# Rotary neighbours by a partition shuffle on VectorE instead of TensorE products

## The reference

```
x <- LN(alpha*x + 1/2*(1+g1)*SwiGLU_1(x*(1+s1)+b1))
x <- LN(alpha*x + (1+g2)*W_o[MoBA heads | GLA heads](x*(1+s2)+b2))
x <- LN(alpha*x + 1/2*(1+g3)*SwiGLU_2(x*(1+s3)+b3))
```

```
half = 8
x1, x2 = xr[..., :half], xr[..., half:]           # xr = x[..., :16]
rot = concat([x1*cos - x2*sin, x2*cos + x1*sin])  # features 16..63 unchanged
```

## Time and profile before

| what | us |
|---|---|
| median of 3 runs | 903.28 |
| the profiled execution | 907.4 |
| its span on the core | 905.6 |
| TensorE busy | 861.6 (95%) |
| VectorE busy | 551.8 (61%) |
| ScalarE busy | 348.0 (38%) |
| input product, first row of MI+1 to last row of level 5 | 326.6 to 421.3 |

### The profile page before, as it was taken

One profiled execution on the slowest core, in us unless ns is written; L12 is line 12 of the kernel. 1 busy time (PEld: TensorE's weight loads), 2 busy tenths in 40 slices (PEclk: granted clock), 3 DMA queues, 4 the chain that ended last, 5 costly groups with the idle time before them and its releaser, 6 DMA issues. The chain is left out here.

```text
span 905.6 us, 17041 instructions
## 1 busy us (share of the span) xinstructions
PE 861.6 (95%) x6857; PEld 756.3 (84%) x6857; DVE 551.8 (61%) x873; ACT 348.0 (38%) x494; POOL 27.8 (3%) x32
## 2 busy tenths in 40 slices
PE   5999999999999999999998999979999999999994
PEld 2488988898999589998666777768699999999993
DVE  1454445455566599685786655763877765555656
ACT  2333333223434455354556443621443223334341
POOL 0000000000000000000000000000200000000002
PEclk9799999999999999999999999989999999999997
DMA  9989888987856563546999999989536555534521
GB/s 318 339 259 290 264 246 243 271 254 200 250 162 201 174 202 96 188 147 200 383 317 330 380 386 340 337 316 275 145 106 174 140 142 155 140 97 134 155 64 58
DMA packets 209028, 200.96 MB, mean 222 GB/s; under 512 B 9601, under 2 KB 161293, under 8 KB 208822
## 3 DMA queue, kind: packets, MB, share of 16 engines
q1 hardware_dynamic: 207556, 196.04, 69.4%
q0 software_dynamic: 704, 2.49, 0.7%
q10 hardware_dynamic: 690, 1.35, 0.5%
HBM read 196.04 MB, written 3.80 MB: 221 GB/s over the span
## 5 line engine op out<-in xcount | busy, mean ns | idle before, releaser
L792 PE MATMUL B<-Hh,wh 128*128 128x320 f32 x864 | 258.9, 313 | 0.1
L1841 DVE TENSOR_TENSOR wl<-raw,wh 128x2048 fp32r<-128x2048 f32 x90 | 206.7, 2298 | 85.7 <-ACT wh L1457 85.4
L793 PE MATMUL B<-Hl,wh 128*128 128x320 f32 x864 | 255.0, 309 | 0.0
L1457 ACT ACTIVATE wh<-raw 128x2048 fp32r<-128x2048 f32 x90 | 172.1, 1913 | 134.4 <-PE B L797 95.5
L792 PEld LDWEIGHTS B<-Hh,wh 128*128 128x128 f32 x864 | 162.2, 188 | 16.9 <-issue 16.2
L793 PEld LDWEIGHTS B<-Hl,wh 128*128 128x128 f32 x864 | 162.3, 188 | 0.3
L797 PE MATMUL B<-Hh,wl 128*128 128x320 f32 x864 | 144.3, 309 | 0.0
L797 PEld LDWEIGHTS B<-Hh,wl 128*128 128x128 f32 x864 | 131.2, 188 | 0.0
L792 PE MATMUL B<-Gh,wh 128*128 128x320 f32 x352 | 104.5, 311 | 0.0
L793 PE MATMUL B<-Gl,wh 128*128 128x320 f32 x352 | 103.7, 309 | 0.0
L1457 ACT ACTIVATE sg<-B 128x320 f32<-128x320 f32 x46 | 20.1, 437 | 194.7 <-PE B L797 184.5
(11 more groups left out here) (290 smaller groups left out, 943.4 us busy)
## 6 DMA issues: line engine op xcount, KB each, us to landing
raw<-in_w_ffn_in SPq DMA_DIRECT2D x88, 512.0 KB, 6.2
raw<-in_w_ada SPq DMA_DIRECT2D x68, 512.0 KB, 4.8
ring<-in_cache_k SPq DMA_DIRECT2D x88, 256.0 KB, 5.2
ring<-in_cache_v SPq DMA_DIRECT2D x76, 256.0 KB, 5.3
raw<-in_w_ffn_out SPq DMA_DIRECT2D x32, 384.0 KB, 3.7
raw<-in_w_mix_in SPq DMA_DIRECT2D x24, 512.0 KB, 4.7
raw<-in_w_ffn_out SPq DMA_DIRECT2D x32, 320.0 KB, 4.3
M<-in_cache_v SPq DMA_DIRECT2D x18, 256.0 KB, 5.7
```

The costliest lines, as they stand in the source:

```text
L792: pe.matmul(out, w, xh[k], start=start and k == 0, stop=False)
L793: pe.matmul(out, w, xl[k], start=False, stop=False)
L1457: return act.activation(out, in_, func, **kw)
L1841: dve.tensor_tensor(dst, raw_view(n), f32(wh[:, wbuf(n), :]), ALU.subtract).then_inc(lo_ready, 1)
```

## The change

The rotation matrix goes from the constants, and with it the eight products `rotate(c)` and their fills. `rope(c)` instead lets VectorE shuffle the block's partitions within each group of 32 (partition i takes i+8 for the first 8, i-8 for the next 8) into `hf`, and multiplies that by a sin table whose first 8 rows have their sign turned. A shuffle is an instruction more for each block. In turns 1 to 4 VectorE's `low` comes before the gates and the rotary work instead of behind them. The keys are turned to rows in gap 6 instead of gap 5, and ScalarE copies them out in turn 6, behind `high`, instead of turn 5.

```diff
+NEIGHBOUR = list(range(8, 16)) + list(range(8)) + list(range(16, 32))
...
-GAPS[1] = [("z", 0), ("z", 1), ("rot", 0), ("rot", 1)]
-for _p in range(1, 4):
-    GAPS[1 + _p] = [("rot", 2 * _p), ("rot", 2 * _p + 1)]
-GAPS[5] = [("nk", t) for t in range(3)]
+GAPS[1] = [("z", 0), ("z", 1)]
+GAPS[6] = [("nk", t) for t in range(3)]
...
-            cos[m], sin[m] = np.cos(ang[m % 8]), np.sin(ang[m % 8])
+            cos[m], sin[m] = np.cos(ang[m % 8]), np.sin(ang[m % 8]) * (-1.0 if m % HD < 8 else 1.0)
...
-            def rotate(c):
-
-                pe.wait_ge(out_read, READ["MI"] + c // 2 + 1)
-                pe.matmul(turn_bank(("rot", c))[:, 0:N], C("rot"), M[:, c, :], start=True, stop=True
-                          ).then_inc(tp_filled, 1)
...
-                if 1 <= n <= 4:
-                    rotate(2 * n - 2)
-                    rotate(2 * n - 1)
-                if n == 5:
+                if n == 6:
                     pe.wait_ge(roped, 8)
                     turn_back("nk", CK)
...
                 if n == 5:
                     act.wait_ge(roped, 8)
                     act_(knew[:, :, :], M[:, CK:CK + HP, S:N]).then_inc(new_ready, 1)
+                    level_exps(1)
+                if n == 6:
                     turned_back("nk", kn)
-                    level_exps(1)
...
             def rope(c):
 
-                wait_fill(("rot", c))
-                dve.tensor_tensor(hf[:, 1, :], tb(("rot", c))[:, 0:N], C("sin"), ALU.mult).then_inc(tp_dve, 1)
+                dve.wait_ge(out_read, READ["MI"] + c // 2 + 1)
+                step(dve.stream_shuffle(hf[:, 1, :], M[:, c, :], NEIGHBOUR))
+                dve.tensor_tensor(hf[:, 1, :], hf[:, 1, :], C("sin"), ALU.mult).then_inc(dve_step, 1)
+                step.k += 1
                 step(dve.tensor_tensor(M[:, c, :], M[:, c, :], C("cos"), ALU.mult))
-                dve.wait_ge(tp_dve, dve_through(FILL_AT[("rot", c)]))
...
             for n in range(12):
+                if 1 <= n <= 4:
+                    low(At(MI + n + 2))
                 if n == 1:
                     gates_in()
...
-                    low(At(MI + n + 2))
+                    if n == 0 or n > 4:
+                        low(At(MI + n + 2))
```

More of the change, by code:

```diff
@@ L288, in shape_constants @@
     parts["eps"] = np.full((P, 1), LN_EPS)
[L289 to L296, removed]
     half = 8
@@ L303, in shape_constants @@
         if m % HD < 16:
-            cos[m], sin[m] = np.cos(ang[m % 8]), np.sin(ang[m % 8])
+            cos[m], sin[m] = np.cos(ang[m % 8]), np.sin(ang[m % 8]) * (-1.0 if m % HD < 8 else 1.0)
+    parts["spare"] = np.zeros((P, 64))
     parts["cos"], parts["sin"] = cos, sin
@@ L462, in landing @@
             return landed_mo[n - MO] if MO <= n < MO + 2 else landed[RING_AT[n] % R]
-        used_up = cst[:, CAT["rot"][0]:CAT["reset"][1]]
+        used_up = cst[:, CAT["spare"][0]:CAT["reset"][1]]
         def page_at(b, j):
```

## The result

| | before | after |
|---|---|---|
| median of the runs timed together, us | 904.96 | 909.59 |
| profiled execution, us | 907.4 | 909.05 |
| its span, us | 905.6 | 907.3 |
| from the gates' product to the first turned page, us | 88.54 | 95.84 |

The ratio is 1.0067, with a 95% interval of 1.0047 to 1.0087. On the 903.28 shown ahead that is 909.3 (907.5 to 911.1); 910.4 had been forecast.

A forecast was written before the change was run, and what follows sets the result against it. TensorE, busy without a gap, was taken to bound the input product, with VectorE nearly full. A 4.4 us later level(0), TensorE's saving included, plus 2.7 for half clock made 7.1 over 903.28: 910.4 us, range 904.5 to 914.5.

The forecast's parts named there:

- TensorE's saving, 4.2 us: Input product: dropping two rotation products in each of four gaps, with their slow entries, spares TensorE 4.2 us.
- The shuffle, 0.52: VectorE's ropes: each shuffle of 128x320 with its wait takes 0.52 us, between bounds of 0.39 and 0.84.
- The pause at MI+5's split, 2.1: TensorE at slot MI+5: a first pause of some 2.1 us for VectorE's split, costing nothing by itself.
- `level(0)` 4.4 later, let go by ScalarE's first tile: Gap 6: level(0) starts at 380.5, 4.4 us later, once ScalarE has emptied the first tile of keys.
- The pause's length, from 374 to 380.5: Gap 6: TensorE waits from about 374 to 380.5 before level(0), a pause of 6.5 us.
- The clock, 2.7: Behind the pause in gap 6: granted clock at half for 5.3 us, losing 2.7 us; bounds 0 and 2.7.
- The sum, 7.1: Whole kernel: 4.4 us of delay plus 2.7 of clock make it 7.1 us slower, 910.4 against 903.28.
- Carried in full to the end: Page stage: a delay or gain at slot MI+11's end reaches the kernel's end in full; rival, hidden, 0.08.
- a stretch from 425 on that is shorter than before: Sign from the page stage: if seen, the claim that the delay carries to the kernel's end is wrong.
- If only VectorE were cheap, 2.3 faster: Input product: with ropes with shuffle of 1.2 us instead of 1.96, 2.3 us faster, 901.0; faster cases together 0.08.
- VectorE keeps pace: Rival, input product: TensorE's saving stays, 899.1, needing ScalarE to empty the bank before rounding or another bank; faster 0.08.

The follow-up runs named there:

- second new order: Changed kernel with keys turned in gap 9 and VectorE's work relisted, masks ahead of splits where that counts; ratio to before 0.9959, stretch 3.91 us shorter.
- kept busy: Changed kernel plus five products nobody reads on TensorE in the pause of gap 6; ratio to before 1.0045, stretch 5.01 us longer.
- keys in gap 5: Changed kernel with the keys turned in gap 5 and copied in turn 5 again; ratio to before 1.0081, stretch 5.37 us longer.
- copy first: Changed kernel with ScalarE's copies of the turned keys ahead of the rounding of MI+8; ratio to before 1.0056, stretch 5.07 us longer.
- keys only: Kernel before with only the keys moved to gap 6 and copied in turn 6 behind the rounding; ratio to before 1.0050, stretch 6.41 us longer.
- keys in gap 7: Changed kernel with keys turned in gap 7 behind level(1) and copied in turn 7; ratio to before 1.0011, stretch 0.78 us longer.

## Why the prediction was right

- **TensorE's saving, 4.2 us.** The second new order, where nothing else is waited for, gives back 3.91. Right, a little high.
- **The shuffle, 0.52.** 0.55 from start to start. The row of a float32 operation on two tensors of the same shape (0.52) was the right neighbour, and the one-source row of 0.39 the wrong one. The Trainium skill ("VectorE: DVE Perf Modes", section "The perf-mode tier table (the rule you actually need)") had it so: a shuffle runs at the plain speed. The trace agrees, with 0.52 for the shuffle's row.
- **The pause at MI+5's split, 2.1.** 2.48. It did bring a fall of the clock, which I had not said, and it cost nothing, as I had: `level(0)` starts at 47.28 with that fall and at 47.27 without it (kept busy), since ScalarE sets the release two slots on.
- **`level(0)` 4.4 later, let go by ScalarE's first tile.** 5.01, with that releaser, and moved by 1.80 when the rounding was taken from ahead of the copy. Of the 0.6 missing, 0.5 are VectorE's: I had `level_diff(1)` end 0.36 later than before, and it ended 0.84 later. The six shuffles make 0.2 of that, and the later high half of MI+4 about 0.15 (its split starts 15.04 behind the gates' product; I had 14.9). The other 0.1 is ScalarE's: 4.23 from `level_exps(1)` to `level(0)` where I had 4.1.
- **The pause's length, from 374 to 380.5.** 4.96 instead of 6.5: TensorE came later than I had it, for the half clock behind the first pause. It made no difference to the time.
- **The clock, 2.7.** 2.29 by the experiment that held it up; the time at half behind the restart was 5.15 us where I had taken 5.3 from the earlier trace rows. Half of that time is more than the loss, since not all of the work doubles: the 16 matmuls of `level(0)` took 2.08 against 1.16, and the slot's products start 0.267 us apart at half clock against 0.147. By the last two figures 5.15 us at half lose 2.3, an estimate that meets the 2.29.
- **The sum, 7.1.** 7.30 in the stretch. That it is so near is in part luck: the release was taken 0.6 too early and the clock 0.4 too dear, and the two errors nearly cancel.
- **Carried in full to the end.** The text named a sign against this: a stretch from 425 on that is shorter than before. It was, by 1.7 us. The other traces show that this is not the page stage hiding a delay. From the first turned page to the end, six kernels whose clock was at half for 6.8 us in all between there and 890 us took nearly the same: 481.75 us with a delay of 0.78, and 481.52, 481.20, 481.45, 481.68 and 481.53 with delays of 5.01 to 7.30 (keys in gap 5, copy first, kept busy, keys only, the changed kernel). Three with 10.2 us at half took 482.91 (2.18 earlier), 483.25 (before) and 483.66 (0.45 later). The other three, with 17.0 to 20.4 us at half, took 483.56 to 485.47. So the difference goes with the time at half clock, if not in proportion, and not with the delay: a delay or a gain is carried.
- **The whole time** moved by 6.1 (4.2 to 7.9, from the ratio), a ratio in which executions with more and with fewer falls of the clock are mixed. Seven of the nine runs of the changed kernel took 909.05 to 909.91, at a mean granted clock of 0.985. Those runs of before (beside the experiments) that had a mean clock of 0.990 or 0.991 took 901.57 to 903.83. The 10.2 us at half that the changed kernel's trace has in the input product are 0.0056 of its span's mean clock, which is the distance between these groups; so the clock was presumably alike elsewhere, and their means, 902.9 and 909.5, lie 6.6 us apart.

"If only VectorE were cheap, 2.3 faster" has not been tried; the run without the shuffle is not it, since two ropes then still take 2.88.

The case "VectorE keeps pace" named what it needed, another bank, and with another gap and order that is what came out.

What part each has can be told at `level(0)`. The moved copy alone starts it 4.17 later (keys only). With the shuffles, the ropes and the new places of the splits `level_exps(1)` comes 0.84 later, and the same 4.23 hang behind it. 4.17 and 0.84 make the 5.01: the two stand one behind the other on one chain. Either is enough to lose what TensorE was spared: with the keys away from the bank VectorE's work turns 4.2 of gain into 0.8 of loss.

## What to carry to other kernels

Work moved from a full engine to one with idle time must fit the deadlines between, not the sum of the idle time: here 4.4 us of shuffles fitted into 5 us of idle time only in the second order tried, with each split, rope and mask placed by when its reader wants it. Where small results pass through banks in turn, the list of fills decides who waits for whom; before moving one, look at which fill gets its bank next and how much stands before its reader. And count a pause of the matrix engine with what comes behind it: here 5.0 us of delay became 7.3 by the half clock, and five useless products took 2.3 of it back.

## What the runs showed of the hardware

A pause of 2.5 us at the same product (the split of MI+5) was followed by a fall of the granted clock in the traces of the changed kernel, of keys in gap 5 and of keys in gap 7, and by none in those of kept busy and copy first. In the changed kernel the fall came 1.0 us after TensorE had restarted at 357.42 (a mean of 0.73 from 358 to 359 puts it at 358.46), so a pause can cost clock when TensorE is busy again. The changed kernel's windows behind that pause:

```profile
358.00:359.00 1.00, 1.00 (x7) 1.00 (x7) 0.96 (x3) 1.00 (x1) 0.00 (x0) 0.73 0.39 49
...
361.00:362.00 1.00, 1.00 (x6) 1.00 (x6) 0.97 (x2) 0.00 (x0) 0.00 (x0) 0.56 0.85 291
```

It was at half for 3.4 us there. Each of the pauses of 4.09 us and more before `level(0)` had a fall in it or at its end, and the pause of 3.64 with keys in gap 5 one behind it.

The same kernel can thus end some us apart from run to run. One place is near 25 us into the kernel (half from 22 to 32 us in the profile of before and of the second new order, full in that of after), another is the page stage. A small change is therefore read better in a stretch of the trace than in the whole time.

A shuffle of 128x320 float32 takes 0.52 us, and loading its pattern, which stands before each one, 0.01.
